# FFN gate and up products: one 512-column product with the high weights against both parts of x

## The reference, cut to what matters

```python
FFN_HIDDEN = -(-8 * D_MODEL // (3 * 256)) * 256      # 2816

def swiglu(h, w_gate, w_up, w_down):
    return (jax.nn.silu(h @ w_gate) * (h @ w_up)) @ w_down
```

## Time and profile before

| | |
|---|---|
| profiled execution, first to last instruction (span) | 1989.6 us |
| the profiled execution's own time | not given apart from its span |
| median of three runs | 1992.52 us (1989.73 to 1992.9) |
| TensorE matmul busy | 1910.4 us, 96% |
| VectorE / ScalarE / GpSimd busy | 1387.8 / 994.2 / 257.6 us |
| granted TensorE clock, mean | 0.990 |
| FFN of layer 0, loop | about 240 to 434 us |
| FFN of layer 1, loop | about 704 to 895 us |

### The profile page before, as it was taken

How to read it: one execution, slowest core, us unless ns; L and a number is a source line. 1 busy time by engine, 2 the same in 40 slices (tenths; PEclk the granted TensorE clock), 3 DMA queues, 4 the chain that set the end, 5 groups by cost and what they waited for, 6 DMA issues and landing times.

```text
span 1989.6 us, 33648 instructions
## 1 busy us (share of the span) xinstructions
PE 1910.4 (96%) x13400; PEld 1763.7 (89%) x13400; DVE 1387.8 (70%) x2518; ACT 994.2 (50%) x1444; POOL 257.6 (13%) x118
## 2 busy tenths in 40 slices
PE   6999899999999999999999899999999999999998
PEld 6887799989978799999998899999988888999997
DVE  5898765658946773338667559988878887666665
ACT  5645544464534554445555455566653334444444
POOL 0001044430001034440000066000000000000000
PEclk9999999999997999999999999999999999999999
DMA  8754477756463355555444354577767866465452
GB/s 319 248 184 154 148 273 247 260 186 224 161 246 133 117 181 190 181 181 196 157 141 170 106 171 169 181 214 217 217 211 253 299 239 231 183 227 197 172 209 106
DMA packets 94522, 392.82 MB, mean 197 GB/s; under 512 B 7680, under 2 KB 41616, under 8 KB 55840
## 3 DMA queue, kind: packets, MB, share of 16 engines
q1 hardware_dynamic: 94368, 390.69, 56.5%
HBM read 372.83 MB, written 15.73 MB: 195 GB/s over the span
## 4 chain that ended last, share of the span: by engine, by line
PE 78%; DVE 11%; ACT 3%; issue 1%; DMA 1%; POOL 0%; DVEq 0%; SPq 0%; ACTq 0%
PE ps L565 10%; PE ps L567 10%; PE ps L566 10%; PE acc L561 9%; PE acc L562 9%; PE acc L563 9%; PE acc L565 3%; PE acc L567 3%; PE acc L566 3%; DVE wlo L1340 2%; PE ps L1295 1%; PE acc L1295 1%; DVE arena L1369 1%; PE ps L710 1%; DVE arena L2240 1%
## 5 line engine op out<-in xcount | busy, mean ns | idle before, releaser
L2388 ACT ACTIVATE whi<-raw 128x1024 fp32r<-128x1024 f32 x559 | 591.1, 1060 | 485.9 <-PE acc L563 276.4
L1340 DVE TENSOR_TENSOR wlo<-raw,whi 128x1024 fp32r<-128x1024 f32 x463 | 571.4, 1241 | 297.0 <-ACT whi L2388 293.7
L565 PE MATMUL ps<-hhi,whi 128*128 128x256 f32 x1848 | 527.3, 285 | 6.6 <-DVE wlo L1340 3.2
L567 PE MATMUL ps<-hhi,wlo 128*128 128x256 f32 x1848 | 522.8, 283 | 0.0
L566 PE MATMUL ps<-hlo,whi 128*128 128x256 f32 x1848 | 522.8, 283 | 0.0
L565 PEld LDWEIGHTS ps<-hhi,whi 128*128 128x128 f32 x1848 | 354.1, 192 | 11.7 <-issue 3.5
L566 PEld LDWEIGHTS ps<-hlo,whi 128*128 128x128 f32 x1848 | 354.2, 192 | 2.8
L567 PEld LDWEIGHTS ps<-hhi,wlo 128*128 128x128 f32 x1848 | 354.1, 192 | 0.0
L1340 POOL TENSOR_TENSOR wlo<-raw,whi 128x1024 fp32r<-128x1024 f32 x96 | 240.1, 2503 | 611.8 <-ACT whi L2388 611.5
L561 PE MATMUL acc<-whi,chi 128*128 128x512 f32 x752 | 296.4, 394 | 3.5 <-DVE wlo L1340 1.9
L562 PE MATMUL acc<-whi,clo 128*128 128x512 f32 x752 | 295.0, 392 | 0.0
(11 more groups left out here) (450 smaller groups left out, 2419.7 us busy)
## 6 DMA issues: line engine op xcount, KB each, us to landing
raw<-in_peer_down SPq DMA_DIRECT2D x64, 1024.0 KB, 5.0
raw<-in_peer_up SPq DMA_DIRECT2D x64, 1024.0 KB, 5.2
arena<-in_ada SPq DMA_DIRECT2D x80, 512.0 KB, 5.0
raw<-in_w_gate SPq DMA_DIRECT2D x22, 1024.0 KB, 4.8
raw<-in_w_up SPq DMA_DIRECT2D x22, 1024.0 KB, 4.8
raw<-in_w_down SPq DMA_DIRECT2D x22, 1024.0 KB, 4.8
arena<-spill SPq DMA_DIRECT2D x14, 1024.0 KB, 7.0
spill<-hT_t SPq DMA_DIRECT2D x22, 448.0 KB, 5.6
```

The costliest lines, as they stand in the source:

```text
L565: e.matmul(out, hi, xh, start=start, stop=False, skip_group_check=True)
L567: i = e.matmul(out, lo, xh, start=False, stop=stop, skip_group_check=True)
L1340: e.tensor_tensor(out=lo, in0=w, in1=hi.bitcast(F32), op=ALU.subtract).then_inc(*X(("lo", j)))
L2388: e.activation(hi, w, ACT.Copy, scale=1.0).then_inc(*self.A(("hi", j)))
```

## The change

Both parts of x lie in one tensor, so that one product moves 512 columns (high x, then low x) past the high weights, and a second one moves high x past the low weights into the first half of the bank. A bank now holds 128 hidden columns in two halves that must be added, so a step takes four banks where it took two. VectorE adds the halves of each bank into SBUF (`ve_halves`), ScalarE's silu reads SBUF, and the multiplication reads SBUF on both sides.

```diff
-        hhi, hlo = sb("hhi", [128, 2048], F32R), sb("hlo", [128, 2048], F32R)
+        hpair = sb("hpair", [128, 4096], F32R)
...
+        self.hP = hpair[:, :].rearrange("p (s a t) -> p a s t", s=2, a=8)
+        self.hH, self.hL, self.cH, self.cL = self.hP[:, :, 0, :], self.hP[:, :, 1, :], tiles8(chi), tiles8(clo)
...
-        self.act = alloc(1024, 4, T)
+        self.act, self.up = alloc(1024, 4, T), alloc(512, 2, T)
...
+    def pe_mm2(self, e, ps, tile, k, *keys):
+        hi, lo, end = tile
+        if end is not None:
+            keys = (*keys, ("used", end))
+        e.matmul(ps.rearrange("p (s t) -> p s t", s=2), hi, self.m.hP[:, k], start=k == 0, stop=False, skip_group_check=True)
+        i = e.matmul(ps[:, 0:T], lo, self.m.hH[:, k, :], start=False, stop=k == 7, skip_group_check=True)
+        if keys:
+            i.then_inc(*self.P(*keys))
...
+    def pe_linear_halves(self, e, name, i, split=None):
+        self.pe_ada(e)
+        if split:
+            for j in range(2):
+                self.banks.take(e, name, i, j)
+        for n in range(16):
+            j, k = (n % 2, n // 2) if split else (n // 8, n % 8)
+            if split and j == 0:
+                self.pe_split(e, split, k)
+            if not split and k == 0:
+                self.banks.take(e, name, i, j)
+            self.pe_mm2(e, self.banks.tile(name, i, j), self.W.tile(e, name, (2 * i + j) * 8 + k), k,
+                        *([("full", name, i, j)] if k == 7 else []))
...
-            self.pe_linear(e, f"w_gate{layer}", i, 8, 2, m.hH, m.hL, None if i else f"ffn{layer}")
-            self.pe_linear(e, f"w_up{layer}", i, 8, 2, m.hH, m.hL)
+            self.pe_linear_halves(e, f"w_gate{layer}", i, None if i else f"ffn{layer}")
+            self.pe_linear_halves(e, f"w_up{layer}", i)
...
+    def ve_halves(self, e, dst, *key):
+        src = self.banks.tile(*key)[:, :].rearrange("p (s t) -> p t s", s=2)
+        e.wait_ge(*self.at("full", *key))
+        e.tensor_reduce(out=dst, in_=src, axis=AX, op=ALU.add, negate=False).then_inc(*self.V(("out", *key)))
...
             self.ve_linear(e, f"w_gate{layer}", i, 8, 2)
             self.ve_linear(e, f"w_up{layer}", i, 8, 2)
-            e.wait_ge(*self.at("out", f"w_gate{layer}", i))
-            e.wait_ge(*self.at("full", f"w_up{layer}", i))
-            pu = self.banks.tile(f"w_up{layer}", i)[:, 0:512].rearrange("p (a t) -> p a t", a=2)
-            e.tensor_tensor(out=m.act[:, s, :], in0=m.act[:, s, :], in1=pu, op=ALU.mult).then_inc(
-                *V(("out", f"w_up{layer}", i)))
+            for j in range(2):
+                self.ve_halves(e, m.act[:, s.start + j, :], f"w_gate{layer}", i, j)
+            for j in range(2):
+                self.ve_halves(e, m.up[:, j, :], f"w_up{layer}", i, j)
+            e.wait_ge(*V.last)
+            e.wait_ge(*self.at("silu", layer, i))
+            e.tensor_tensor(out=m.act[:, s, :], in0=m.act[:, s, :], in1=m.up, op=ALU.mult).then_inc(*V(("act", layer, i)))
...
-            e.wait_ge(*self.at("full", f"w_gate{layer}", i))
-            if i >= 2:
-                e.wait_ge(*self.at("lo", f"act{layer}", i - 2))
-            e.activation(m.act[:, s, :], self.banks.tile(f"w_gate{layer}", i)[:, :].rearrange("p (a t) -> p a t", a=2),
-                         ACT.Silu, scale=1.0).then_inc(*A(("out", f"w_gate{layer}", i)))
-            e.wait_ge(*self.at("out", f"w_up{layer}", i))
+            e.wait_ge(*self.at("out", f"w_gate{layer}", i, 1))
+            e.activation(m.act[:, s, :], m.act[:, s, :], ACT.Silu, scale=1.0).then_inc(*A(("silu", layer, i)))
+            e.wait_ge(*self.at("act", layer, i))
```

More of the change, by code:

```diff
@@ L300, in tiles8 @@
             return ap[:, :].rearrange("p (a t) -> p a t", a=8)
-        self.hH, self.hL, self.cH, self.cL = tiles8(hhi), tiles8(hlo), tiles8(chi), tiles8(clo)
+        self.hP = hpair[:, :].rearrange("p (s a t) -> p a s t", s=2, a=8)
+        self.hH, self.hL, self.cH, self.cL = self.hP[:, :, 0, :], self.hP[:, :, 1, :], tiles8(chi), tiles8(clo)
         self.hT = tiles8(self.hT_t)
```

## The result

The changed kernel took 2029.32 us (median of 4 runs, 2024.82 to 2033.23) beside 1991.12 us for the kernel before in the same session (1989.19 to 1992.9): a ratio of 1.0194, 95% interval 1.0177 to 1.0212. It is slower by 1.9%.

What follows compares the result with a forecast made beforehand. The FFNs were taken as bound by TensorE's issue pace, with little spare in the chain across engines. 22.7 (layer 1) + 5.4 (layer 0) + 3.2 (clock) - 8.8 (saving) = +22.5 on 1992.5: 2015.0 us, range 2001 to 2030.

Steps and rivals of the forecast that it cites:

- steady chain of layer 1: Reductions behind VectorE's low part of d1 make TensorE wait 1.6 us before gates 4 to 10: seven steps, 11.2 us.
- Bank waits of 3.2: Layer 1, steps 0 and 2: TensorE waits 3.2 us each inside up for the first reduction to free a bank.
- The third 3.2 us: Layer 1, step 1: VectorE, already fully booked, gets four more reductions and delays TensorE by 3.2 us.
- Gate rows: After layer 1's step 10, VectorE's gate rows come 1.85 us later; TensorE, already waiting for them, loses 1.9 us more.
- Layer 1 in sum: Layer 1's waits in all: 3.2 x 3 + 11.2 + 1.9 = 22.7 us.
- Reductions: VectorE's four 128x512 reductions from PSUM a step: 0.69 us each, starts 0.60 apart, bounds half and double.
- Half and double the price: Rivals: reductions at 0.35 us, chain 1.1 us shorter, 2000 us (near no change: chance 0.06); double, 2037 us, chance 0.04.
- Layer 0: Waits of 5.4 us: 2.7 for step 0's bank, 0.5 each in steps 2, 5, 10, 0.4 after steps 2, 4, 6.
- bank wait of step 0: Layer 0, step 0: TensorE waits from 249.7 to 252.3 and a little for a bank, 2.7 us.
- GpSimd gets in first: Rival: in layer 0 VectorE's delayed low part waits 2.1 us behind GpSimd's, four times: +8.4, 2023.4 us; chance 0.14.
- Clock: Four waits of 2.7 to 3.2 us bring two falls to half clock of 1.6 us: 3.2 us, bounds 0 and 6.4.
- Saving: In 704 FFN tiles one 512-column product replaces two of 256: 0.3475 for 0.360 us, 12.5 ns each, 8.8 us in all.

Runs made afterwards that it cites:

- run 1: Changed kernel with VectorE's two gate reductions moved ahead of up's ada piece and low parts: 2000.2 us, ratio 1.0047 to the kernel before.
- run 2: Changed kernel with layer 1's low parts swapped between VectorE and GpSimd, so VectorE has g0, u0, d0: 2007.97 us, 1.0077 to the kernel before.
- run 4: Changed kernel with each reduction replaced by a copy of the bank's first half (256 elements), second half not added: 2017.01 us, 1.0122 to the kernel before.
- Run 6: Changed kernel with x's high and low parts adjacent for each tile, so the 512-column moving operand is one run: 2032.02 us, 1.0194 to the kernel before.
- Run 7: Changed kernel with two tiles' products ordered 512, 512, 256, 256 columns, all but the first gate: 2030.75 us in a single execution.
- run 9: Changed kernel with only gate paired, gate reductions early, up as in the kernel before: 1985.1 us, ratio 0.9975 to the kernel before.
- run 8: Changed kernel with gate reductions early, second up tile summed in its bank as before, multiplication in two parts: 2000.69 us, 1.0047 to the kernel before.

## Why the prediction was right, and where it was off

**Direction and main mechanism: right, and shown.** That the time lies in the range is partly luck: it is 0.7 us inside the upper end. (The chances that the range leaves out sum to 0.18, not 0.17.) The steady chain of layer 1 was predicted at 1.6 us and came at 1.43 to 1.52 in seven places (runs 1 and 2 remove it in two ways). Bank waits of 3.2 came at 3.07 in step 0 (731.92) and 3.06 in step 2 (770.25). The third 3.2 us, for VectorE's queue in step 1, came as 0.55 ahead of step 1's up and 2.32 ahead of gate 2, both released by GpSimd's low part. Gate rows: 1.9 predicted, 1.88 (2.64 for 0.76). Layer 1 in sum: 22.7 predicted, 21.2 measured.

**Reductions: right.** One takes 0.68 us, and four take 2.48 with 0.60 between their starts. Half and double the price are both far off; at half price the chain would have been 3 x 0.30 + 0.35 = 1.25 us shorter, not 1.1.

**Layer 0: the wrong branch.** Predicted 5.4 us, measured 13.6. The bank wait of step 0 was right (2.7, measured 2.50). The step that failed is the rival "GpSimd gets in first", which I gave 0.14 with the argument that VectorE's operation ahead is still running and its next one queued right behind. That was the situation, and GpSimd won it: its low part has its start at 294.38, within VectorE's operation that runs to 294.78, and VectorE's queued one waited. The trace of before held the same case, one operation later. There GpSimd's low part of the earlier trace rows started while VectorE's low part was running, and the piece queued on VectorE behind that was held up until GpSimd was done:

```profile
287.29 3.49 DVE L1369 SCALAR_TENSOR_TENSOR arena<-arena,gs_t 128x512 f32<-128x512 f32 x2
```

It took 3.49 us where the same two operations take 1.54, and GpSimd's low part ended at 289.45 within it. The predicted waits of 0.4 before steps 3, 5 and 7 became 2.46, 2.47 and 1.56 (the last for the small operation of the piece, L1386, that such a low part held up), and one of 2.30 came ahead of step 1's up, near where the rival had it. The bank waits of 0.5 in steps 2, 5 and 10 were 0.40, 0.35 and 0.40. The gate rows of layer 0 (1.16) weren't foreseen at all, and they are the same mechanism: before, VectorE's small operation L1472 started 0.27 us ahead of GpSimd's low part (426.24 and 426.51) and took 0.17 us; now it starts 0.27 behind (444.24 and 443.97) and takes 2.21. The rival's four waits were priced at 8.4 us and measured 7.6 more than the branch that I took; that 13.6 - 5.4 comes to 8.2 is because the gate rows' 1.16 is in it and the bank waits came 0.55 short. The Trainium skill's rule (SBUF — State Buffer, "Who interferes with whom"), that whoever issues first holds the shared access for the whole instruction, agrees with these rows and should have had more weight than my argument from the queue.

**Clock: a size off.** I predicted two falls of 1.6 us; measured are six stretches with some 11 us. They came with waits of 2.3 to 3.1 us, shorter than the 3.47 that I had from before, and one of them, with the 3.06 at 770.25, lasted 6.8 us. In run 4 one followed a wait of 2.02. Waits of 2.32 had been harmless in the one row that I took as the lower end; one row was thin. Not each such wait is followed by a fall: in the changed kernel those of 2.50 and 2.30 us (255.23 and 266.28) were not, and in run 1 three waits of 2.62, 2.49 and 2.47 us left one fall. What decides is open.

**Saving: a size off.** It was 6.2 us instead of 8.8. In the faster rhythm the sum of the two prices was right (0.3467 us, where I had 0.3475); the term that was mis-sized is the rest of the stretches, at 0.3533, which no row of before could show. Run 6 excludes the two runs of the operand as the cause. Run 7 shows that the order of long and short products matters, but not how, and what sets the rhythm is open. By the Trainium skill's fixed part of 2.5 ns a product (TensorE: Matmul & The Clock Gate, "Wait — 56ns, not 53.3ns?") the saving would be 1.8 us, an estimate from that page; the measured 6.7 and 13.3 ns a tile don't agree with that either.

The errors add up: +8.2 for layer 0's waits, +8 for the clock, +2.6 for the saving and +4 for restarts, which the prediction had left out; -1.5 in layer 1's waits and -2.0 in stages outside the FFNs. That is 19 us, as the spans have it (41.8 against 22.5). The medians differ by 38.2, since the profiled execution of the changed kernel was its slowest; so the predicted time was 14 us low.

## What to carry to other kernels

When an operation is added to an engine that is idle two thirds of the time in that stage, count what its place in that engine's order costs, not its share: the same reductions cost 29 us less when half of them stood ahead of an operation that waits. Where two engines meet on shared access within a few tenths of a microsecond, work out who arrives first after the change, and count a queued operation as late. Try the half of a change that has room: with the gate reductions early, gate alone gains 0.25%, where gate and up together lose 0.5% (run 1).

## What the hardware showed that was not expected

- GpSimd's low part got the access while VectorE had an operation of its own running and the next one queued; VectorE's then took 3.39 us instead of 1.22. A lead of 0.23 or 0.24 us (before, run 9) or a lag of 0.31 (the changed kernel, run 8) decided it.
- Products of alternating length, 512 and 256 columns, run in two rhythms in the same kernel, 0.3467 or 0.3533 us a pair, each for a whole stretch. 0.3467 is what the two cost among their like once a row of products has settled (0.2267, over 851 products from 1470 us on in the kernel before, and 0.120). One run or two in the moving operand gives the same two values. In the order 512, 512, 256, 256 the pair takes 0.3483 throughout.
- Half clock came with waits of 2.3 to 3.1 us (2.02 in run 4) in the middle of a stage that otherwise keeps TensorE busy, in stretches of 3.4 or 6.8 us. In the changed kernel six waits with 16 us in all cost 11 us more that way.
- A reduction of 128x512 from PSUM took 0.68 us also beside a low part of GpSimd (run 9: 294.82, GpSimd's from 294.72 to 297.16), while a multiplication of 128x256 with both inputs in SBUF went from 0.42 to 2.13 us beside one (run 8).
